# Reordering the first layer's opening and the last output tile of a four-layer trunk on eight cores

## What is computed

```
h    = rmsnorm(x, pre_g)                                   # 2176 tokens x 1024
proj = h @ w_in                                            # 1024 -> 6400: u v z_a p z_b xc bg cg z_c
a    = u * (tril(w_s) @ rmsnorm(v, v_g) + b_s) * silu(z_a) # chunks of 128 tokens, 6 heads
b    = pool_scale * ((window_mean(p) - p) @ w_pg) * silu(z_b)
c    = bg * conv3(cg * xc) * silu(z_c)
x    = x + rmsnorm(concat(a, b, c) @ w_out, post_g)        # 2048 -> 1024
```

## Time and profile before

| what | us |
|---|---|
| time, median of 3 runs | 2047.11 (2046.69 to 2047.9) |
| the profiled execution's own time | 2047.11 |
| its span, slowest core | 2046.0 |
| spans of cores 0, 1, 4, 5 | 2046.0, 2045.2, 2045.6, 2046.0 |
| spans of cores 2, 3, 6, 7 | 2017.9, 2017.9, 2016.6, 2019.4 |
| PE busy on core 0 | 2017.1 (99%) |

### The profile page before, as it was taken

One profiled execution on the slowest core, in us unless ns is written; L12 is line 12 of the kernel. 1 busy time (PEld: TensorE's weight loads), 2 busy tenths in 40 slices (PEclk: granted clock), 3 DMA queues, 4 the chain that ended last, 5 costly groups with the idle time before them and its releaser, 6 DMA issues.

```text
span 2046.0 us, 32524 instructions; the slowest of 8 cores (2016.6 to 2046.0 us)
## 1 busy us (share of the span) xinstructions
PE 2017.1 (99%) x10731; PEld 999.6 (49%) x10942; DVE 1092.4 (53%) x1604; ACT 590.5 (29%) x1131; POOL 323.2 (16%) x688
## 2 busy tenths in 40 slices
PE   8999999999999999999999999999999999999998
PEld 4444444444454554444455455444445455444443
DVE  5654455555556555555556555555454745555433
ACT  6431122223333112222333312222333321222211
POOL 5300011012230001002222000111223100110011
PEclk9888899999999999999999999999999999999999
DMA  8421254358614224437733223551861432343243
GB/s 224 78 51 27 32 91 68 57 105 224 169 38 70 45 48 78 70 62 163 207 114 62 53 41 63 81 82 32 222 201 51 73 68 36 53 67 57 75 152 134
DMA packets 123720, 185.28 MB, mean 91 GB/s; under 512 B 63010, under 2 KB 68770, under 8 KB 123556
## 3 DMA queue, kind: packets, MB, share of 16 engines
q0 software_dynamic: 41040, 71.39, 23.9%
q1 hardware_dynamic: 82516, 111.79, 18.5%
HBM read 198.79 MB, written 42.35 MB: 118 GB/s over the span
## 4 chain that ended last, share of the span: by engine, by line
PE 97%; DMA 1%; issue 1%; POOL 0%; DVE 0%; ACT 0%; DVEq 0%; POOLq 0%; ACTq 0%; SPq 0%
PE ps L487 64%; PE ps L862 23%; PE ps L591 8%; PE ps L769 1%; DMA sb_ring<-w_v 1%; PE ps L735 1%; DMA sb_wout<-x_in 0%; PE ps L560 0%; POOL sb_stats L480 0%; DVE sb_ar L460 0%; POOL sb_ring L419 0%; DVE sb_ar L464 0%; DVE sb_mix L464 0%; POOL sb_stats L478 0%; ACT sb_ar L456 0%
## 5 line engine op out<-in xcount | busy, mean ns | idle before, releaser
L487 PE MATMUL ps<-sb_hT,sb_ring 128*128 128x512 bf16 (+1 forms) x6898 | 1341.9, 351 | 11.8 <-DVE sb_ar L464 3.8
L487 PEld LDWEIGHTS ps<-sb_hT,sb_ring 128*128 128x128 bf16 x7040 | 634.8, 99 | 664.6 <-issue 83.7
L456 ACT ACTIVATE sb_ar<-ps 128x512 f32<-128x512 f32 (+2 forms) x508 | 288.8, 569 | 754.0 <-PE ps L487 555.8
L862 PE MATMUL ps<-sb_wout,sb_mix 128*128 128x512 bf16 x2132 | 468.0, 379 | 2.3
L862 PEld LDWEIGHTS ps<-sb_wout,sb_mix 128*128 128x128 bf16 x2176 | 212.9, 98 | 256.7
L412 POOL DMA_DIRECT2D sb_ring<-w_t x176 | 94.9, 542 | 1004.5 <-PE ps L487 598.4
L460 DVE TENSOR_TENSOR sb_ar<-ps,sb_ar 128x512 f32<-128x512 f32 (+1 forms) x240 | 145.6, 607 | 170.3 <-PE ps L487 166.0
L464 DVE SCALAR_TENSOR_TENSOR sb_ar<-sb_pcx,sb_convw,sb_ar 128x512 f32<-128x512 f32 x192 | 144.3, 751 | 92.3 <-ACT sb_ar L835 82.3
L591 PE MATMUL ps<-sb_ring,sb_hT 128*128 128x512 bf16 (+1 forms) x1065 | 180.4, 327 | 4.6 <-DVE sb_hbuf L464 2.1
L456 ACT ACTIVATE sb_pcx<-ps 128x512 f32<-128x512 f32 (+2 forms) x133 | 108.0, 812 | 259.7 <-PE ps L862 200.3
L460 DVE TENSOR_TENSOR sb_pcx<-ps,sb_ar 128x512 f32<-128x512 f32 x96 | 66.4, 692 | 207.5 <-PE ps L487 204.0
(11 more groups left out here) (80 smaller groups left out, 627.8 us busy)
## 6 DMA issues: line engine op xcount, KB each, us to landing
sb_ring<-w_t POOLq DMA_DIRECT2D x176, 256.0 KB, 5.4
x_mid<-sb_ar SPq DMA_DIRECT2D x51, 512.0 KB, 3.4
sb_ar<-x_mid SPq DMA_DIRECT2D x51, 512.0 KB, 5.0
sb_wout<-w_out POOLq DMA_DIRECT2D x64, 256.0 KB, 9.1
sb_ar<-x_in SPq DMA_DIRECT2D x20, 512.0 KB, 5.6
y_o<-sb_ar SPq DMA_DIRECT2D x16, 512.0 KB, 3.2
sb_ring<-w_v POOLq DMA_DIRECT2D x32, 192.0 KB, 13.2
sb_wout<-x_in SPq DMA_DIRECT2D x8, 512.0 KB, 8.1
```

The source lines that it names most:

```text
L456: return emit(ACT, lambda a: a.activation(out=out, in_=in_, func=func, scale=scale, **kw), reads=reads, writes=writes)
L487: ins = pe.matmul(bank(b, n), lhsT=wa.ap[:, k, :], rhs=hT[:, k, c0:c0 + n], start=(k == 0), stop=(k == 7))
L862: ins = pe.matmul(bank(b + half), lhsT=mix[:, k, j * 128:(j + 1) * 128], rhs=wout[:, k, half * 512:(half + 1) * 512], start=(k == 0), stop ...
```

## The change

There are two separate pieces. In the planner the due times of `sq`, `rs` and `h` are four units before the begin of their v product from tile 5 on (before: one for tile 5, three from tile 6 on); `T` of tile 5 no longer waits for v of tile 4, and v of tile 4 now waits for `T` of tile 5; the transposes from tile 5 on use banks 0 and 1 (before: 2 and 3), and the v products from tile 3 on rotate over bank pairs 6, 2, 4 (before: 6, 0, 4). Beside that, the x loads from tile 5 on wait for the sixth piece of w_v in place of the fifth. At the end, the last output tile is made as 768 and 256 columns, and its final sum in three parts of 448, 384 and 192 columns, stored by SP, ACT and SP.

```diff
-    norm = [begin[i] - (3.0 if i > 5 else 1.0 if i == 5 else 0.0) for i in range(NT)]
+    norm = [begin[i] - (4.0 if i >= 5 else 0.0) for i in range(NT)]
...
-        add(("T", i), "P", .47, [("h", i)] + ([("v", max(i - 2, 4))] if i > 4 else []), begin[i] - 1.9, 11.0)
+        add(("T", i), "P", .47, [("h", i)] + ([("v", i - 2)] if i > 5 else []), begin[i] - 1.9, 11.0)
...
-                + ([("T", i + 1)] if 5 <= i < NT - 1 else []), begin[i])
+                + ([("T", i + 1)] if 4 <= i < NT - 1 else []), begin[i])
...
-            return [6 + n[1] % 2 if n[1] < 5 else 2 + n[1] % 2]
+            return [6 + n[1] % 2 if n[1] < 5 else n[1] % 2]
         if n[0] == "v" or n[0] == "vp" and n[2] == 0:
-            b = 2 * n[1] if n[1] < 3 else (6, 0, 4)[n[1] % 3]
+            b = 2 * n[1] if n[1] < 3 else (6, 2, 4)[n[1] % 3]
...
+        def last_parts(b):
+
+            return ((0, 768, 512 * b), (768, D, 512 * ((b + 2) % 8)))
...
-                for half in range(2):
-                    emit(PE, lambda pe: f(pe, (half,)), reads=rd, writes=[bank_res[b + half]])
+                for c0, c1, p in last_parts(b):
+                    def g(pe):
+                        for k in range(16):
+                            for q in range(c0, c1, 512):
+                                n = min(512, c1 - q)
+                                ins = pe.matmul(ps[:, p + q - c0:p + q - c0 + n],
...
-            for i in range(2):
-                stt(x[:, hs[i]], ar[:, tm + i, :], c0, x[:, hs[i]], ALU.mult, ALU.add,
-                    reads=[rx[i], R_ar[tm + i], R_stat[s2[0]]], writes=[rx[i]])
-                sp_dma(dst[:, hs[i]], x[:, hs[i]], [rx[i]], [], d_xst[j] if i else d_xl)
+            for i, (q0, q1) in enumerate(((0, 448), (448, 832), (832, D))):
+                rq = Res()
+                stt(x[:, q0:q1], tmp[:, q0:q1], c0, x[:, q0:q1], ALU.mult, ALU.add,
+                    reads=rx + R_ar[tm:tm + 2] + [R_stat[s2[0]]], writes=[rq])
+                emit(ACT if i == 1 else SP, lambda h: h.dma_start(out=dst[:, q0:q1], in_=x[:, q0:q1]),
+                     reads=[rq], dsem=(d_xl, d_xst[j], d_vs)[i])
...
         for j in range(5, NT):
-            load_x0(j, toks_of([kres[4]]))
+            load_x0(j, toks_of([kres[5]]))
```

More of the change, by code:

```diff
@@ L853, in c_stage, with banks_of @@
             sp_dma(nsc_s[l], samp[:, 0:6 * SB * 10], [R["samp"]], [], d_out)
+        def last_parts(b):
+            return ((0, 768, 512 * b), (768, D, 512 * ((b + 2) % 8)))
+        def banks_of(p, n):
+            return [bank_res[i] for i in range(p // 512, (p + n - 1) // 512 + 1)]
         def out_mm(l, j):
@@ L869, in out_mm @@
             else:
-                for half in range(2):
-                    emit(PE, lambda pe: f(pe, (half,)), reads=rd, writes=[bank_res[b + half]])
+                for c0, c1, p in last_parts(b):
[4 more added lines that the diff above has]
+                                ins = pe.matmul(ps[:, p + q - c0:p + q - c0 + n],
+                                                lhsT=mix[:, k, j * 128:(j + 1) * 128], rhs=wout[:, k, q:q + n],
+                                                start=(k == 0), stop=(k == 15))
+                        return ins
+                    emit(PE, g, reads=rd, writes=banks_of(p, c1 - c0))
             return b
@@ L894, in out_ew @@
             s2 = [alloc_stat(), alloc_stat()]
-            hs = [slice(0, 512), slice(512, 1024)]
-            for i in range(2):
-                tok = act(jnk[:, hs[i]], bank(b + i), AF.Square, reads=[bank_res[b + i]], writes=[rj, R_stat[s2[i]]],
+            for i, (q0, q1, p) in enumerate(last_parts(b)):
+                n = q1 - q0
+                src, br = ps[:, p:p + n], banks_of(p, n)
+                tok = act(jnk[:, q0:q1], src, AF.Square, reads=br, writes=[rj, R_stat[s2[i]]],
                           scale=float(D) ** -0.5, accum=stats[:, s2[i]:s2[i] + 1])
-                emit(DVE, lambda v: v.tensor_tensor(out=ar[:, tm + i, :], in0=bank(b + i), in1=post_bc[:, hs[i]],
-                                                    op=ALU.mult),
-                     reads=[bank_res[b + i], R["post"]], writes=[R_ar[tm + i]], extra=[tok])
+                tmp = ar[:, tm:tm + 2, :].rearrange("p a b -> p (a b)")
+                emit(DVE, lambda v: v.tensor_tensor(out=tmp[:, q0:q1], in0=src, in1=post_bc[:, q0:q1], op=ALU.mult),
+                     reads=br + [R["post"]], writes=[R_ar[tm + i]], extra=[tok])
             c0, c1 = (stats[:, i:i + 1] for i in s2)
```

## The result

The changed kernel took 2017.49 us (median; 2016.83 to 2017.84); the kernel before, run beside it, 2046.69 to 2047.9. The ratio is 0.9854, 95% interval 0.9837 to 0.9872. The forecast of 2045.3 was wrong, and so was its range: what came is the third rival, 2019 us, to which I gave a chance of 0.04. Executions in which the clock was lowered for hundreds of microseconds or on a whole die came with every kernel, the two pairs of cores of such a die often some 25 us apart even without the stop, and are left out of all numbers here; the others are called undisturbed.

A forecast was written before the change was run, and what follows sets the result against it. PE's chain of waits and the cores with the 0.81 stretch were taken to bound the kernel; core 4's terms -3.46 + 1.4 + 0.3 + 0.5 - 0.1 = -1.4 gave span 2044.2, time 2045.3 us, range 2041.3 to 2048.5.

The forecast's parts named there:

- the third rival: The 0.81 stretch goes away since its cores begin stage B without a stop: 2019 us, chance 0.04.
- the sum's base: Terms were added to the profiled spans of cores 0 and 4, 0.81 stretch included; slowest core decides: 2044.2 + 1.1 us.
- the stretch of 0.81: Core 0's clock granted 0.81 from 88 to 240 us; the four cores with it were taken to set the time.
- the first term: PE's wait before stage B removed: gain 3.46 us, plus 1.4 of clock on core 0 only.
- the gap of 3.81: PE's 3.81 us wait before stage B's first product, for bank 0 held by v of tile 16.
- The prediction's last sign: If the slow stretch changes length, the forecast's sum says nothing.
- The gap and its half clock: Before stage B: two products fill 3.46 of 3.81 us, third waits 0.35; half clock cost core 0 1.4, core 4 nothing.
- The new order of the opening: First layer's opening: PE waits before T 5 and v 4, so v 5 starts 1.4 us later; bounds -0.4 to 1.6.
- The hand-over from POOL to DVE: Behind h 5, vn 0 waits for POOL's power, so T 5 starts no earlier than before, at 33.39 us.
- The later loads: x loads from tile 5 wait for w_v's sixth piece: x 5 lands 0.3 us later, bounds -0.3 to +1.3.
- The end: Last tile: squares gain 0.2 us, three-part sum costs a little more; together -0.1 us, bounds -0.3 to +0.3.
- the clock after the new gap: PE's stop before T 5 and v 4 costs clock: 0 to 1.4 us, taken as 0.5.

The follow-up runs named there:

- nine-stop kernel: Kernel before with stage B in bank 2 and the new end, plus nine PE stops before stages B, A, C of layers 1 to 3: 2076.41, 2076.12, 2075.87 us.
- kernels with bank 2: Kernel before with layer 0's stage B starting in bank 2 instead of 0: alone 2014.88 us; with the changed kernel's end 2015.05 and 2014.86 us.
- first comparison: Changed kernel beside the kernel before, on a chip not on record: 2017.49 us against 2046.69 to 2047.9 us.

## Why the prediction was wrong

**The step that failed** is the sum's base. I took the stretch of 0.81 as a property of cores 0, 1, 4 and 5 that would stay, and let it set the end ("the four cores with this slow stretch set the time"). It hung on the very stop that the first term took away: with the stop 15 of 30 executions on chip D had a late pair, without it 0 of 20, and the changed kernel's cores have 1.00 from 88 to 240 us. The profile had the hint, and the prediction named it: the stretch comes soon after the gap of 3.81. I set two observations against it, and neither holds. "Later layers begin stage B at 1.00": they do so without a stop, so they were no counter-example but the other half of the evidence. "Core 2, with the same program, has no such stretch": the stop makes the stretch possible, not certain, as core 2 of the nine-stop kernel shows; a core that escapes proves nothing. Three times between 2046.69 and 2047.9, by their length all with it, made it look fixed. The third rival's price was near, 2019 against 2017.49, though it left out what the change itself gains; its chance should have been several times larger. The prediction's last sign fits what came: "if the slow stretch changes length, the sum says nothing".

**The Trainium skill** ("TensorE: Matmul & The Clock Gate", section Part 1) sets the onset of its current limit within about 5 to 20 us of a third core of the die starting dense matmuls. The size agrees: here 0.81 begins within 9 us of a core's own restart; which core of the die was the third is not shown, since each core's times count from its own begin. That the limit takes a whole die and holds while the load lasts does not agree: core 0 of the nine-stop kernel was back at 1.00 from 912 us under full load, and core 2 of the same die stayed at 1.00 in that stretch.

**The other terms**, against executions without the stretch:

- The gap and its half clock: forecast -3.46 - 1.4 on core 0 and -3.46 on core 4, measured -5.5 to -6.0 in the kernels with bank 2, where all of the 3.81 us goes. The two products did take the place of the wait, and the third waits 0.3 us, as forecast. The half clock was undersized: 5.5 to 6.0 less 3.81 is 1.7 to 2.2, and filling the stop gave 1.7 to 1.9. The cores differ: core 2 of before, from 73 to 81 us, lost 0.43 of the 5.97 us that PE was busy, 2.6 us, where core 0 lost 1.4.

```profile
73.00:81.00 8.00, 5.97 (x15) 0.57 0.84 150
```

- The new order of the opening: forecast +1.4 and +0.5 for the clock, measured +1.1 for both, the third product's 0.3 included. On core 0 v of tile 5 starts 36.24 - 31.50 = 4.74 us after the transpose of tile 5, forecast 4.56, before 3.19. The hand-over from POOL to DVE, on which the term rests, is there with its 0.53 us.
- The later loads: forecast +0.3, bounds -0.3 to +1.3, measured +2.1 across two chips, 1.4 by chip B: beyond the upper bound. I took the landing of a typical load; the end is set by the core whose load lands last. There the clock goes down too: on core 2 v of tile 4 took 5.03 - 2.76 = 2.3 us longer, more than the 1.4 that I had as the most for the clock after the new gap.
- The end: forecast -0.1, measured 0.0. The squares and the sums have the lengths I took (0.39 and 1.5):

```profile
2011.09 0.38 ACT L456 ACTIVATE sb_pcx<-ps 128x256 bf16<-128x256 f32 x1 [0.84 <-PE ps L882]
```

```profile
2012.86 1.54 DVE L464 SCALAR_TENSOR_TENSOR sb_ar<-sb_ar,sb_stats 128x448 f32<-128x448 f32 x3 [0.76 <-POOL sb_stats L921]
```

The sum for a core without the stretch was forecast as -2.8 (core 0), and -2.8 was measured on chip C. That is luck: the half clock and the opening came out better than forecast, the loads worse by about as much. Of the 29.6 us of the first comparison some 3 are the change's work and 26 to 27 the stretch.

**A version that beats both**: the kernel before with stage B in bank 2 and the new end, 2014.86 us on chip D, 3 us below the changed kernel on its distance to before (-6.0 against -2.8); ratio to all undisturbed executions of before, late pairs included, 0.9933, interval 0.9887 to 0.9978. The new end adds nothing that shows; bank 2 alone took 2014.88 on chip B.

## What to carry to other kernels

A stop of PE before dense work can cost far more than its length: look at the granted clock in the stretch behind it, and where a slow stretch follows a stop that the change removes, give the case that the stretch goes with the stop a chance of its own, and price it. A core that does the same and escapes is no counter-example for something that happens by chance; ask where it ever happens without the cause. For a term that every core pays with its own size, take the slowest core, not the typical one.

## What the runs showed of the hardware

In undisturbed executions a granted clock of 0.81 for some 161 us came on pairs of neighbouring cores, never or always by the chip or the occasion (0 of 20 to 4 of 4 executions of one kernel), within 9 us of a restart of dense products (two traces), and went away under full load. The two cores of the pair went together: spans of 2100.6 and 2101.2 against 2073.0. A stop of 2.08 us already cost five of the eight cores half their clock for a few microseconds (12.65 against 10.97 us for the same products), and filling a stop of 3.81 us with useless matmuls made the kernel 1.9 us faster.
